# Two attention stages: splitting weight chunks by Pool-issued transfers and a GpSimd negation in place of ScalarE and VectorE

## The reference, cut to what matters

```python
def dilated_layer(x, c, kv_groups, ada_w, ada_b, norm_g, w_in, q_norm_g, w_out):
    ...
    h = rms_norm(x, norm_g) * (1 + scale) + shift
    qz = h @ w_in                       # 1024 x 4096: 24 query heads of 128, and a gate z of 1024
    q = qz[..., :N_Q_HEADS * HEAD_DIM].reshape(bsz, s, N_Q_HEADS, HEAD_DIM)
    z = qz[..., N_Q_HEADS * HEAD_DIM:]
    q = rms_norm(q, q_norm_g) * (HEAD_DIM ** -0.5)
    # three dilation groups of 8 heads, banded softmax attention in each, then a softmax over the groups
    ...
    y = o.reshape(bsz, s, B_WIDTH) * jax.nn.silu(z)
    return x + gate * (y @ w_out)
```

```python
    proj = u @ w_in                     # its last 2048 columns are the gates g
    y_a = chunked_attention(q, k, v, rel_table) @ w_attn_out      # 8 heads of 64
    y_b = conv_module(c_in, ...) @ ...                            # depthwise convolution of width 31, layer norm, silu
    gates = jax.nn.sigmoid(g + gate_bias)
    merged = gates[..., :D_MODEL] * y_a + gates[..., D_MODEL:] * y_b
```

## Time and profile before

| | |
|---|---|
| median of 3 runs | 1925.88 us (1925.7 to 1926.75) |
| span of the profiled execution | 1924.0 us |
| PE busy | 1830.6 us (95%) |
| DVE busy | 1047.5 us (54%) |
| ACT busy | 736.8 us (38%) |
| GpSimd busy | 53.2 us (3%) |

### The profile page before, as it was taken

The page is one execution under the profiler, slowest core; times in us unless marked ns, Lnnn a source line. Parts: engine busy times, 40 slices in busy tenths (PEclk is TensorE's granted clock), DMA queues, the critical chain, the costliest instruction groups (busy, mean ns, idle before and its releaser), DMA issues.

```text
span 1924.0 us, 22231 instructions
## 1 busy us (share of the span) xinstructions
PE 1830.6 (95%) x8618; PEld 1492.9 (78%) x8618; DVE 1047.5 (54%) x1498; ACT 736.8 (38%) x1008; POOL 53.2 (3%) x103
## 2 busy tenths in 40 slices
PE   4999999989999999999999999998999999999998
PEld 3788888856877777778888887986666788888887
DVE  6336666458566666754444314699775463333213
ACT  4445554224355656432323214223462342323212
POOL 1000001000000000100000000000000000000000
PEclk8999999989999999999999999999999999999999
DMA  8346565422322221233342323232223223342321
GB/s 329 134 131 188 176 176 174 150 77 67 86 66 66 66 61 50 70 104 90 88 125 82 119 89 88 88 110 70 63 66 110 88 69 106 87 119 78 121 88 66
DMA packets 246679, 201.10 MB, mean 105 GB/s; under 512 B 6386, under 2 KB 225860, under 8 KB 245572
## 3 DMA queue, kind: packets, MB, share of 16 engines
q1 hardware_dynamic: 238048, 166.25, 29.3%
q0 software_dynamic: 8064, 33.56, 5.0%
q10 hardware_dynamic: 484, 0.16, 0.0%
HBM read 197.83 MB, written 2.11 MB: 104 GB/s over the span
## 4 chain that ended last, share of the span: by engine, by line
PE 77%; DVE 13%; ACT 5%; issue 3%; DMA 1%; DVEq 0%; SPq 0%; POOL 0%; ACTq 0%; POOLq 0%
PE acc L699 13%; PE acc L701 13%; PE acc L700 13%; PE sc L1064 6%; DVE s_s_row L2163 4%; PE acc L1064 3%; DVE s_w_low L1827 2%; PE tr L1064 2%; ACT s_w_high L1323 2%; PE ob L1064 2%; PE misc L1064 2%; DMA s_ada_w<-in_a_ada_w 1%; PE sc L699 1%; PE sc L701 1%; PE sc L700 1%
## 5 line engine op out<-in xcount | busy, mean ns | idle before, releaser
L1827 DVE TENSOR_TENSOR s_w_low<-s_raw,s_w_high 128x2048 fp32r<-128x2048 f32 (+1 forms) x149 | 337.2, 2263 | 356.4 <-ACT s_w_high L1323 356.4
L1323 ACT ACTIVATE s_w_high<-s_raw 128x2048 fp32r<-128x2048 f32 x151 | 284.6, 1885 | 205.0 <-PE acc L1064 174.6
L699 PE MATMUL acc<-s_h_high,s_w_high 128*128 128x512 f32 x880 | 345.1, 392 | 1.6 <-DVE s_sg L2399 1.6
L701 PE MATMUL acc<-s_h_high,s_w_low 128*128 128x512 f32 x880 | 342.5, 389 | 0.0
L700 PE MATMUL acc<-s_h_low,s_w_high 128*128 128x512 f32 x880 | 342.5, 389 | 0.0
L699 PEld LDWEIGHTS acc<-s_h_high,s_w_high 128*128 128x128 f32 x880 | 165.3, 188 | 37.2 <-issue 4.1
L701 PEld LDWEIGHTS acc<-s_h_high,s_w_low 128*128 128x128 f32 x880 | 165.2, 188 | 34.6
L700 PEld LDWEIGHTS acc<-s_h_low,s_w_high 128*128 128x128 f32 x880 | 165.3, 188 | 33.7 <-issue 0.2
L1699 ACT ACTIVATE s_hid_high<-s_hd 128x512 fp32r<-128x512 f32 x44 | 27.8, 632 | 219.3 <-DVE s_hd L2408 119.0
L890 PE MATMUL acc<-s_h_high,s_w_high 128*128 128x512 f32 x256 | 107.3, 419 | 2.2 <-DVE s_w_low L1827 1.4
L699 PE MATMUL acc<-s_b_high,s_w_high 128*128 128x512 f32 x224 | 91.7, 410 | 11.3 <-DVE s_b_low L1876 7.3
(11 more groups left out here) (446 smaller groups left out, 3353.7 us busy)
## 6 DMA issues: line engine op xcount, KB each, us to landing
s_raw<-in_a_w_in SPq DMA_DIRECT2D x48, 512.0 KB, 5.0
s_raw<-in_ffn_w_gate SPq DMA_DIRECT2D x44, 512.0 KB, 4.0
s_raw<-in_ffn_w_up SPq DMA_DIRECT2D x44, 512.0 KB, 5.2
s_raw<-in_ffn_w_down SPq DMA_DIRECT2D x40, 512.0 KB, 4.2
s_raw<-in_w_in SPq DMA_DIRECT2D x36, 512.0 KB, 4.4
s_raw<-in_b_w_in SPq DMA_DIRECT2D x32, 512.0 KB, 4.8
s_ada_w<-in_b_ada_w POOLq DMA_DIRECT2D x24, 512.0 KB, 4.9
s_ada_w<-in_a_ada_w POOLq DMA_DIRECT2D x8, 1024.0 KB, 12.6
```

The costliest lines, as they stand in the source:

```text
L699: pe.matmul(bank[b][:, :], w_high[:, o:o + P], hi, start=(k == 0), stop=False, skip_group_check=grouped)
L701: mm = pe.matmul(bank[b][:, :], w_low[:, o:o + P], hi, start=False, stop=(k == nk - 1), skip_group_check=grouped)
L1323: act.activation(w_high[:, part], raw[:, part], ACT.Copy).then_inc(w_high_ready, 1)
L1827: dve.tensor_tensor(w_low[:, w], raw[:, w], w_high[:, w].bitcast(F32), ALU.subtract).then_inc(w_ready, 1)
```

## The change

It concerns 22 chunks: numbers 1 to 15 of "qz" and 1 to 7 of "gates" (`BY_QUEUE`). For these, ACT's copy and DVE's subtraction are gone. GpSimd waits until the chunk has landed and the slot is free, issues a transfer inside SBUF that casts `raw` to `w_high`, multiplies `raw` by -1 into `w_low` (rounding to fp32r), waits for its own multiplication, and issues a second transfer, which adds `raw` to `w_low`. The matmuls and SP's next load wait for both transfers by new semaphores (`high_cast`, `low_added`) in place of `w_ready`. The counts of `w_ready` and `w_high_ready` for all other chunks are corrected for the missing ones. The calls for the first chunk of the following stages stay on ACT and DVE (in "gates" at rows 28 and 29). `tile_sum` now stands between gates chunks 3 and 4 in GpSimd's program.

```diff
+BY_QUEUE = [C0["qz"] + j for j in range(1, 16)] + [C0["gates"] + g for g in range(1, 8)]
+def by_engines(c):
+    return c + 1 - sum(m <= c for m in BY_QUEUE)
+def slot_use(c):
+    return sum(m <= c and m % 2 == c % 2 for m in BY_QUEUE)
...
             def wait_slot(q, s):                       # SP
-                if not isinstance(q, int) or q > 0:
-                    sp.wait_ge(x_landed, 16 * TT)
-                    sp.wait_ge(w_ready, 2 * q + s - 1)
+                before = 2 * q + s - 2
+                if isinstance(q, int) and q == 0:
+                    return
+                sp.wait_ge(x_landed, 16 * TT)
+                if isinstance(q, int) and before in BY_QUEUE:
+                    sp.wait_ge(high_cast[s], 16 * slot_use(before))
+                    sp.wait_ge(low_added[s], 16 * slot_use(before))
+                elif isinstance(q, int):
+                    sp.wait_ge(w_ready, by_engines(before))
+                else:
+                    sp.wait_ge(w_ready, 2 * q + (s - 1 - moved))
...
+            def by_queue(c, tiles):                    # GpSimd
+                s = c % 2
+                w = slice(s * SLOT, (s + 1) * SLOT)
+                pool.wait_ge(w_landed[s], 32 * (c // 2) + 32)
+                pool.wait_ge(tile_ready, tiles)
+                pool.dma_start(w_high[:, w], raw[:, w]).then_inc(high_cast[s], 16)
+                pool.tensor_scalar(w_low[:, w], raw[:, w], -1.0, None, ALU.mult).then_inc(low_turned, 1)
+                pool.wait_ge(low_turned, BY_QUEUE.index(c) + 1)
+                pool.dma_start(w_low[:, w], raw[:, w], accum_op=ALU.add).then_inc(low_added[s], 16)
+            for j in range(1, 16):
+                by_queue(C0["qz"] + j, T0["qz"] + 2 * (j - 1))
...
-            tile_sum()
+            for g in range(1, 8):
+                if g == 4:
+                    tile_sum()
+                by_queue(C0["gates"] + g, T0["gates"] + 2 * (g - 1))
...
             def chunk(c):                              # PE
-                pe.wait_ge(w_ready, c + 1)
+                if isinstance(c, int) and c in BY_QUEUE:
+                    pe.wait_ge(high_cast[c % 2], 16 * slot_use(c))
+                    pe.wait_ge(low_added[c % 2], 16 * slot_use(c))
+                elif isinstance(c, int):
+                    pe.wait_ge(w_ready, by_engines(c))
+                else:
+                    pe.wait_ge(w_ready, c + (1 - moved))
...
-                    if t is not None and t % 2 == 0 and t < 4 * NQ - 2:     # ACT, first attention
-                        next_high(q0 + t // 4, t // 2 % 2, t0 + t)
...
-                if n % 4 == 0:                                              # ACT, second attention
+                if n == H2 * TT - 4:
                     next_high(q0 + n // 8, n // 4 % 2, t0 + n // 2)
...
-                    if low is not None:                                     # DVE, first attention
-                        next_low(*low)
-                        low = None
...
-                if n % 4 == 1:                                              # DVE, second attention
+                if n == H2 * TT - 3:
                     next_low(q0 + n // 8, n // 4 % 2)
```

More of the change, by code:

```diff
@@ L84 @@
 HALF_CHUNKS = {C0[name] + c for name in ("dn1", "dn2") for c in range(2)}
+BY_QUEUE = [C0["qz"] + j for j in range(1, 16)] + [C0["gates"] + g for g in range(1, 8)]
[3 more added lines that the diff above has]
+    return sum(m <= c and m % 2 == c % 2 for m in BY_QUEUE)
+MOVED_QZ, MOVED_GATES = 15, len(BY_QUEUE)
 def crossed(name, t):
@@ L329, in build @@
         w_high_ready, w_ready = sem("w_high_ready"), sem("w_ready")
+        high_cast = [sem("high_cast0"), sem("high_cast1")]
+        low_turned, low_added = sem("low_turned"), [sem("low_added0"), sem("low_added1")]
         tile_ready = sem("tile_ready")
@@ L448, in _ @@
         def _(sp):
+            moved = 0
             def wait_slot(q, s):
-                if not isinstance(q, int) or q > 0:
-                    sp.wait_ge(x_landed, 16 * TT)
-                    sp.wait_ge(w_ready, 2 * q + s - 1)
+                before = 2 * q + s - 2
[9 more added lines that the diff above has]
+                    sp.wait_ge(w_ready, 2 * q + (s - 1 - moved))
             def column(n0):
@@ L549, in _ @@
             q0 = C0["bo"] // 2
-            with sp.Fori(0, 2) as i:
+            for i in range(2):
                 for s in range(2):
                     chunk_wide(i + q0, s, W["b_out"], i * 512 + s * 2 * P)
+            moved = MOVED_QZ
             def ffn(l, post, pre=None):
@@ L582, in _ @@
             q0 = C0["gates"] // 2
-            with sp.Fori(0, 4) as i:
+            for i in range(4):
                 for s in range(2):
@@ L586, in _ @@
                     chunk_paired(i + q0, s, W["in2"], n0, W["in2"], n0 + D)
+            moved = MOVED_GATES
             q0 = C0["outs"] // 2
@@ L668, in _ @@
                                    pattern=[[-1, P]], channel_multiplier=1).then_inc(dist_ready, 1)
+            def by_queue(c, tiles):
[9 more added lines that the diff above has]
+                by_queue(C0["qz"] + j, T0["qz"] + 2 * (j - 1))
             for s in range(2):
-                pool.wait_ge(w_high_ready, C0["bo"] + s + 1)
+                pool.wait_ge(w_high_ready, by_engines(C0["bo"] + s))
                 w = slice(s * SLOT, (s + 1) * SLOT)
@@ L1821, in _ @@
             own = Chain(dve, dve_own)
+            moved = 0
             def low_part(q, s):
-                dve.wait_ge(w_high_ready, 2 * q + (s + 1))
+                if isinstance(q, int):
+                    dve.wait_ge(w_high_ready, by_engines(2 * q + s))
+                else:
+                    dve.wait_ge(w_high_ready, 2 * q + (s + 1 - moved))
                 w = slice(s * SLOT, s * SLOT + chunk_width(q, s))
@@ L2245, in _ @@
                         scale(*before)
-                    if low is not None:
-                        next_low(*low)
-                        low = None
                     if n == 3:
@@ L2262, in _ @@
                         y_rest(s - 2)
-                    if t is not None and t % 2 == 0 and t < 4 * NQ - 2:
-                        low = q0 + t // 4, t // 2 % 2
             scale(a - 1, 3)
@@ L2292, in low_of_x @@
                    .then_inc(h_ready, 1)
-            dve.wait_ge(w_ready, C0["bo"] + 2)
+            dve.wait_ge(w_ready, by_engines(C0["bo"] + 1))
             for i in range(KD):
```

## The result

The changed kernel takes 1946.46 us (median of 4 runs, 1945.35 to 1949.54), beside 1926.32 us (1925.7 to 1927.85, 4 runs) of the kernel before on the same chip: ratio 1.0105, 95% interval 1.0092 to 1.0118. That is slower by 1.05%, 20 us. The forecast was 1909, in a range of 1900 to 1938, with a chance of 0.29 for slower.

What follows compares the result with a forecast made beforehand. PE, busiest but not full, was taken to wait for ACT and DVE, delayed by weight splitting. Gains of 14.6 us (first attention) and 1.9 (second) off the 1924.0 span gave 1907.5, so a median of 1909, range 1900 to 1938.

Steps and rivals of the forecast that it cites:

- the two waits of a head: First attention: PE waits about 1.25 us for ACT's squares and 0.78 us for DVE's reciprocal roots; both should go.
- The waits were the weights': Rival, chance 0.07: DVE, ACT and PE's round trip may keep the waits without the splitting of weights; 1925 us.
- PE's idle time: Both attentions: 19.2 and 10.5 us idle; moving work between the other engines can win these 29.7 us and no more.
- the 16.5: First attention: gain of 3.66 + 10.15 + 2.69 us from waits that go, if nothing new is late.
- The chunk path: From slot free to both transfers landed: 4.2 + 9.0 = 13.2 us, bounds 8.6 and 18.3; only chunk 2 late, by 1.9.
- The rival with 1935: Chance 0.28: adds land after 12.6 us, the chunk path becomes 16.8 us, and PE waits in front of chunks A.
- what GpSimd does to DVE: Both attentions: each negation can hold a DVE scaling, or a tap with two SBUF inputs, for up to 3 us.
- the cover is what the removed work leaves: First attention: holds priced at nothing; the row after chunk A starts 0.7 us late, against some 2.4 us earlier without copy and subtraction.
- 1.6 and 1.1 us in the second: Second attention: chunks 2 and 3 among taps cost 1.6 us; holds of scalings at chunks 4 to 7 cost 1.1.
- priced at 1.9 us won: Second attention: 1.9 us won at chunk 1 and 2.7 at chunks 4 to 7, less the holds, sum 1.9 us.
- The rival of held DVE: Chance 0.14: a negation of 4.58 us holds the scaling behind chunk A, the 1.25 us waits stay; 1924 us, no change.
- the clock is no part of this: Both attentions: the granted clock was read as 0.99 and 1.00, so it was left out of the forecast.

Runs made afterwards that it cites:

- ACT's negation: Against the changed kernel, ACT makes the negation in place of GpSimd, and both transfers stay on GpSimd's queue: 1906.05 us, ratio 0.9892 to the kernel before.
- the kernel with four pieces: Against the changed kernel, GpSimd's negation is cut into four instructions of 512 columns without gaps: 1911.89 us, ratio 0.9920 to the kernel before.

## Why the prediction was wrong

What bounds the kernel was read rightly. With ACT's negation, and so with no hold by GpSimd, the two waits of a head go. A head takes 31.4 us (forecast 31.9), the first attention gains 18.1 us (forecast 14.6, up to 16.5) and the second 7.1. The waits were the weights', so that rival falls. But PE's idle time was no ceiling for the gain: of the 18.1 us only 14.7 are idle time, and 3.4 are PE's own busy time (245.69 to 242.25 us for the same matmuls, at a granted clock of 0.99 in both). Part of it may be this: the record of a matmul is 0.39 us long, but the next one starts after 0.23, so ahead of each wait some 0.16 us count as busy. For the 13 waits that went that is 2 us, an estimate from these rows; the rest stays open. And the wait of 1.08 us for ACT in the last head, counted among the 16.5, is still there (1.1).

The chunk path was 13.2 us by the working, and came out at 0.56 + 5.40 + 0.3 + 7.1 = 13.4. That it was right was luck: two errors cancel, a negation 2.3 us too short and an add 1.9 us too long. PE's waits in front of chunks are 3.2 us in all, before chunks 1, 2 and 3, and none stands before a later chunk. That margin held because the heads stayed as long as before; with the faster heads of the kernel with four pieces it was gone. The rival with 1935, which put the loss here, came nearest in time and had the wrong cause.

The step that failed is the one on what GpSimd does to DVE. It knew the hold from the earlier trace rows and gave it a price of nothing in the first attention, since "the cover is what the removed work leaves", and of 1.6 and 1.1 us in the second. Three things were wrong in it:

1. The size. The hold of a scaling is as long as what is left of the negation. With 3.1 us the scaling behind chunk A would have been late by 0.7; with 5.40 it was held 3.7, more than the cover of 2.4 us. The 3.1 came from a select, an instruction of another kind. The upper bound of 4.58 came from a subtraction, on the thought that two inputs cannot be faster than one. That was no bound.
2. The count. Only chunk A was looked at. Chunk B's negation held the scaling of 192 columns just as long (3.9 us on average). Twelve of the fifteen negations held a scaling, all but the first three, which run ahead of the first scaling: 44 us in all, 3.7 us each, more than the 2.3 of the subtraction that was removed. DVE was not relieved at all. Likewise in the second attention six of seven held something: scalings took 16 us and taps 7 us more, 3.8 us for each of the six.
3. The second attention, priced at 1.9 us won, lost 17.4. The rival of held DVE named the mechanism and came to 1924 with 4.58 us. But it put the second attention at neither gain nor loss. The forecast had counted a hold of 1.1 us on average for each of chunks 4 to 7; each met a scaling that then took 4.0 to 4.8 us, and PE's waits grew to 3 us.

What no part of the prediction had is the clock: 7.4 of the 17 us are PE's own work, longer at the lower clock behind such waits. The clock was read as 1.00 in this stage before and taken as given ("the clock is no part of this").

## What to carry to other kernels

Before a GpSimd instruction is called free, lay it over DVE's timeline: which two-input or fast DVE instructions would start while it runs, and what waits behind them. Then choose its length and place. Cut into quarters, the same negation turned a loss of 20 us into a gain of 15. A subtraction of 4.6 us in its place, begun some 5 us later, gave a gain of 12, though it lost in one attention half of what it won in the other. A wait of PE can cost more than its length, by the clock behind it: here 0.4 of it more for one of 4.9 us, and 0.8 of it more in the second attention, where the waits for the scaling grew to 3 us.

## What the runs showed that I had not expected

- GpSimd's negation of 128x2048 with one input took 5.40 us, longer than its subtraction with two, 4.58 to 4.60; a quarter of it took 1.53 to 1.55. Its memset took 1.84.
- A transfer of 1 MB inside SBUF landed in 4.3 to 6.3 us as a cast and in 6.9 to 7.3 as an add (medians of the kernels), so the add is not twice as dear as the cast. The add's issue took 0.87 to 0.93 us on GpSimd, the cast's 0.53 to 0.57.
- Behind PE's waits of 3.04 us (changed kernel, 1340.54) and 4.93 us (ACT's negation, 525.61), matmuls stood 0.43 us apart in place of 0.23; the granted clock of the 8 us with such a wait was 0.79 or 0.89. The first attention of the changed kernel has this once too, behind a wait of 2.12 us at 595.90. In the kernel with ACT's negation it lasted from 525.6 to 530.9, at a granted clock of 0.51, the lower of the two levels, 1.2 and 2.4 GHz.
- A held tap got in before the negation was over (1.2 us before its end it was done), while a tap that met GpSimd's subtraction ended 0.55 us after it. Why the two differ stays open.
